# Most of the modulation weights moved from the prologue to beside the first products and the feed-forward, and the norms' roots taken per token and spread through PSUM

## The reference, cut to what matters

```python
def rmsnorm(x, g):
    return x * rsqrt(mean(x * x, axis=-1) + EPS) * g

m = silu(cond) @ ada_w + ada_b                  # ada_w is 1024 x 6144, per layer
sh1, sc1, g1, sh2, sc2, g2 = split(m, 6)
h = rmsnorm(x, norm1) * (1 + sc1) + sh1
x = x + g1 * mixer(h)       # layer 0: gated DeltaNet and pooling, layer 1: Hyena
h = rmsnorm(x, norm2) * (1 + sc2) + sh2
x = x + g2 * conv_glu(h)
...
def conv_glu(h):                                # ffn_up is 1024 x 5632
    a, gte = split(h @ ffn_up, 2)
    a = dwconv_grid(a, ffn_conv_w) + ffn_conv_b
    return (gelu(a) * gte) @ ffn_down
```

## Time and profile before

| | us |
|---|---|
| median of three runs | 4694.48 |
| lowest and highest | 4691.84, 4698.06 |
| the profiled execution | 4689.33 |
| its span, first to last instruction | 4687.5 |

### The profile page before, as it was taken

How to read it: one execution, slowest core, us unless ns; L and a number is a source line. 1 busy time by engine, 2 the same in 40 slices (tenths; PEclk the granted TensorE clock), 3 DMA queues, 4 the chain that set the end, 5 groups by cost and what they waited for, 6 DMA issues and landing times.

```text
span 4687.5 us, 50772 instructions
## 1 busy us (share of the span) xinstructions
PE 4110.0 (88%) x21784; PEld 3429.5 (73%) x21784; DVE 2458.4 (52%) x2646; ACT 1017.6 (22%) x1384; POOL 1178.8 (25%) x586
## 2 busy tenths in 40 slices
PE   6699888778697999999959999996677799999998
PEld 3488777777475888888747777775566588888886
DVE  1466155555416444455447666579992454444453
ACT  1234122211213111111133333311111311111112
POOL 1221133333233222222231000012231422222224
PEclk8799799999798999999979999998888899999999
DMA  9511000000111111111122222232221011111111
GB/s 351 206 52 37 33 1 1 1 1 1 72 37 36 37 41 36 41 36 37 36 78 65 83 80 87 80 144 83 100 111 36 23 37 36 37 37 41 38 39 63
DMA packets 265336, 280.44 MB, mean 60 GB/s; under 512 B 9221, under 2 KB 221142, under 8 KB 261623
## 3 DMA queue, kind: packets, MB, share of 16 engines
q1 hardware_dynamic: 265112, 277.18, 17.5%
HBM read 219.48 MB, written 57.67 MB: 59 GB/s over the span
## 4 chain that ended last, share of the span: by engine, by line
PE 70%; DVE 19%; DMA 4%; issue 3%; ACT 2%; POOL 1%; SPq 1%; POOLq 0%; DVEq 0%; ACTq 0%
PE PS L590 52%; DVE piece L1470 8%; PE PS L1538 5%; DVE piece L1019 3%; DMA piece<-in_l_ada_w 2%; PE PS L990 2%; PE PS L991 2%; PE PS L986 2%; DVE piece L516 2%; PE PS L1711 1%; PE PS L702 1%; DMA piece<-hyena_tokens 1%; DVE piece L1406 1%; DVE piece L509 1%; DVE piece L1879 0%
## 5 line engine op out<-in xcount | busy, mean ns | idle before, releaser
L590 PE MATMUL PS<-piece,piece 128*128 128x512 f32 (+1 forms) x13824 | 2757.3, 361 | 150.7 <-POOL piece L534 94.5
L590 PEld LDWEIGHTS PS<-piece,piece 128*128 128x128 f32 x13824 | 2304.4, 190 | 600.7 <-issue 160.7
L573 POOL TENSOR_TENSOR piece<-piece,piece 128x1024 fp32r<-128x1024 f32 (+1 forms) x204 | 504.7, 2475 | 2417.9 <-ACT piece L567 2417.9
L1538 PE MATMUL PS<-piece,piece 128*128 128x256 f32 x1920 | 441.3, 392 | 126.1 <-DVE piece L2165 110.8
L1406 DVE SCALAR_TENSOR_TENSOR piece<-piece,piece,piece 128x1024 f32<-128x1024 f32 x352 | 534.9, 1520 | 12.6
L1538 PEld LDWEIGHTS PS<-piece,piece 128*128 128x128 f32 x1920 | 376.4, 197 | 186.1 <-DVE piece L2165 113.6
L1426 DVE SCALAR_TENSOR_TENSOR piece<-PS,piece,piece 128x1024 f32<-128x1024 f32 x224 | 187.7, 879 | 415.0 <-PE PS L590 415.0
L567 ACT ACTIVATE piece<-piece 128x1024 fp32r<-128x1024 f32 (+1 forms) x204 | 205.1, 1007 | 671.4 <-PE PS L590 634.5
L1019 DVE TENSOR_TENSOR piece<-piece,PS 128x512 f32<-128x512 f32 x288 | 185.3, 684 | 249.6 <-PE PS L991 192.3
L1403 DVE TENSOR_SCALAR piece<-piece,piece 128x1024 f32<-128x1024 f32 x44 | 35.7, 812 | 482.4 <-ACT piece L1367 482.4
L1125 POOL TENSOR_TENSOR piece<-piece,piece 128x512 f32<-128x512 f32 x120 | 159.8, 1345 | 123.9 <-PE PS L986 123.2
(11 more groups left out here) (206 smaller groups left out, 3719.1 us busy)
## 6 DMA issues: line engine op xcount, KB each, us to landing
piece<-in_l_ada_w SPq DMA_DIRECT2D x24, 2048.0 KB, 18.1
piece<-in_l_ffn_up SPq DMA_DIRECT2D x88, 512.0 KB, 3.7
piece<-in_l_w_in SPq DMA_DIRECT2D x44, 512.0 KB, 3.8
piece<-in_l_ffn_down SPq DMA_DIRECT2D x48, 384.0 KB, 3.0
piece<-filters_s SPq DMA_DIRECT2D x8, 2176.0 KB, 10.5
filters_s<-piece SPq DMA_DIRECT2D x64, 256.0 KB, 2.0
hyena_tokens<-piece SPq DMA_DIRECT2D x24, 640.0 KB, 4.0
piece<-hyena_tokens SPq DMA_DIRECT2D x12, 1280.0 KB, 5.7
```

The lines of the kernel that those rows point to most:

```text
L573: eng.tensor_tensor(LO[i % 2][0][:, 0:n], RAW[i % raws][:, 0:n], HI[i % 2][1][:, 0:n], ALU.subtract)\
L590: m = eng.matmul(PS[:, bank + b, 0:n], w, x[:, a:a + n], start=first and n_ == 0, stop=last and n_ == 2)
L1538: m = eng.matmul(PS[:, bank, o * HC:(o + 1) * HC], M[i][o], rhs[i], start=i == 0, stop=i == 1)
```

## The change

**Modulation.** The prologue handles only the four tiles of 512 columns that the first norm needs (shift and scale of layer 0's first part), each behind a token tile of x (2, 5, 7, 9). The next 18 halves of 256 columns (the rest of layer 0 and the first of layer 1) are handled in the first seven tiles of the first mixer, three to a tile: behind its steps 0, 3 and 5 TensorE multiplies one half and turns the half before. ScalarE copies the rows out, SyncE loads into two buffers. The last 44 quarters of 128 columns (the rest of layer 1) are handled in the feed-forward of layer 0, one in each "a" and "g" tile: the rows behind step 1, the turn behind step 6. ScalarE's copy of a quarter's rows stands at the head of its work for that item. The feed-forward's weight ring goes from two raw buffers to one, in both layers. In the first mixer's queue on SyncE the first two weight loads no longer wait for the prologue.

**Norms.** In `norm`, TensorE sums the squares per token (ten matmuls of one column into bank 6), root and reciprocal run on 128 x 10, VectorE multiplies the identity by them to ten diagonal blocks, and TensorE multiplies ones by these, which leaves the reciprocals of all tokens on all partitions, in PSUM, where the multiplies read them. `first_norm` takes the place of the first call: ScalarE squares each token tile of x as it lands and VectorE reduces it, so that the sums per token need no matmuls; its remaining steps are those of `norm`.

```diff
+            SQX = [r.take(D) for _ in range(2)]
...
+                eng.wait_ge(ac.sem, ac.at("square", t))
+                eng.tensor_reduce(SS[:, t:t + 1], SQX[t % 2], AX.X, ALU.add).then_inc(*ve.did("sum", t))
...
             def high_channels(eng, t):
+                eng.wait_ge(s_x[t % slots], 16 * (t // slots + 1))
+                if t >= 2:
+                    eng.wait_ge(ve.sem, ve.at("sum", t - 2))
+                eng.activation(SQX[t % 2], XR[t % slots], ACT.Square).then_inc(*ac.did("square", t))
...
+        NA, LANES = 4, 4
+        ADA_BEHIND = (2, 5, 7, 9)
...
+                for t in ((0, 1, 2), (3, 4, 5), (6, 7), (8, 9))[n]:
+                    x_fetch(sp, t)
+                src = A["l0_ada_w"].rearrange("(p k) n -> p k n", k=KD)[:, :, n * 512:(n + 1) * 512]
...
+            for t in range(NT):
+                x_turn(pe, t)
+                if t in ADA_BEHIND:
+                    n = ADA_BEHIND.index(t)
+                    rows(n)
+                    if n:
+                        columns(n - 1)
+            columns(NA - 1)
...
+            ve.tensor_tensor(MOD[:, 0, 0:16], PS[:, 4, 0:32].rearrange("p (m j) -> p m j", j=2), bcast(vec("l0_ada_b", 0, 16), 2), ALU.add)\
+                .then_inc(*veM.did("mod"))
+            ve.wait_ge(veM.sem, veM.at("mod"))
+            ve.tensor_scalar(SCALE_A[:, 0], MOD[:, 0, 8:16, :], 1.0, None, ALU.add).then_inc(*veM.did("plus"))
+            ve.wait_ge(veM.sem, veM.at("plus"))
+            ve.tensor_tensor(SCALE_A[:, 0], SCALE_A[:, 0], bcast(vec("l0_norm1", 0, 8), 2), ALU.mult).then_inc(*veM.did("scale"))
+            ve.tensor_copy(SCALE_A[:, 4], bcast(vec("final_norm", 0, 8), 2)).then_inc(*veM.did("last"))
...
-            RS = r.take(N)
+            DIAG, SS, RS = r.take(NT, P), SQ[1][:, 0:NT], psum(3, N)
...
+                for t in range(NT):
+                    m = eng.matmul(PS[:, 6, t:t + 1], SQ[0][:, t * P:(t + 1) * P], ones[:, 0:1], start=True, stop=True)
+                m.then_inc(*pe.did("sum"))
+                eng.wait_ge(ve.sem, ve.at("diag"))
                 for b, (a, n) in enumerate(CHUNKS):
-                    m = eng.matmul(PS[:, b, 0:n], ones, SQ[0][:, a:a + n], start=True, stop=True)
-                m.then_inc(*pe.did("sum"))
+                    m = eng.matmul(PS[:, 3 + b, 0:n], ones, DIAG[:, a // P:(a + n) // P, :].rearrange("p t c -> p (t c)"), start=True, stop=True)
+                m.then_inc(*pe.did("spread"))
...
-                eng.wait_ge(pe.sem, pe.end())
-                eng.activation(RS, psum(0, N), ACT.Sqrt, scale=1.0 / D, bias=eps).then_inc(*ac2.did("root"))
+                eng.wait_ge(pe.sem, pe.at("sum"))
+                eng.activation(SS, PS[:, 6, 0:NT], ACT.Sqrt, scale=1.0 / D, bias=eps).then_inc(*ac2.did("root"))
...
-                eng.reciprocal(RS, RS).then_inc(*ve.did("inv"))
+                eng.reciprocal(SS, SS).then_inc(*ve.did("inv"))
                 eng.wait_ge(ve.sem, ve.at("inv"))
+                eng.tensor_tensor(DIAG, over(ident, NT), bcast(SS, P), ALU.mult).then_inc(*ve.did("diag"))
+                eng.wait_ge(pe.sem, pe.at("spread"))
...
+        def first_norm(prev, shift, early):
+
+            T = [Region(W_AT + i * N, W_AT + (i + 1) * N).take(N) for i in range(4)]
+            DIAG = Region(FIX_AT - N, FIX_AT).take(NT, P)
+            RS = psum(3, N)
...
+            NB, PER, ADA_TILES = 2 * (13 - NA), 3, 7
+            BW = [Region(W_AT + 5248 + 2048 * i, W_AT + 5248 + 2048 * (i + 1)).take(KD, 256) for i in range(2)]
+            BR = [Region(W_AT + 9344 + 256 * i, W_AT + 9344 + 256 * (i + 1)).take(256) for i in range(2)]
...
+            def fetch_half(eng, h):
+                if h >= 2:
+                    eng.wait_ge(peB.sem, peB.at("rows", h - 2))
+                layer, m = divmod(NA + h // 2, 12)
+                at = m * 512 + h % 2 * 256
+                eng.dma_start(BW[h % 2], A[f"l{layer}_ada_w"].rearrange("(p k) n -> p k n", k=KD)[:, :, at:at + 256]).then_inc(s_aw[h % 2], 16)
+
+            def half_rows(eng, h):
+                eng.wait_ge(s_aw[h % 2], 16 * (h // 2 + 2))
+                if h >= 2:
+                    eng.wait_ge(acBr.sem, acBr.at("rows", h - 2))
+                for k in range(KD):
+                    lane = k % LANES
+                    m = eng.matmul(PS[32 * lane:32 * lane + 32, 6 + h % 2, 0:256], CW[:, k, :], BW[h % 2][:, k, :], start=k < LANES, stop=k >= KD - LANES)
+                m.then_inc(*peB.did("rows", h))
+
+            def half_columns(eng, h):
+                eng.wait_ge(acBr.sem, acBr.at("rows", h))
+                for j in range(2):
+                    c = 256 + 4 * (h // 2) + 2 * j
+                    m = eng.matmul(PS[:, 6 + h % 2, c:c + 2], BR[h % 2][:, j * P:(j + 1) * P], SEL, start=True, stop=True)
+                m.then_inc(*peBt.did("turn", h))
+
+            def half_leaves(eng, h):
+                eng.wait_ge(peB.sem, peB.at("rows", h))
+                if h >= 2:
+                    eng.wait_ge(peBt.sem, peBt.at("turn", h - 2))
+                eng.activation(BR[h % 2], PS[:, 6 + h % 2, 0:256], ACT.Copy).then_inc(*acBr.did("rows", h))
...
-                ended(eng, *before_norm)
                 for i, (kind, g, at) in enumerate(tiles):
                     ring.load(eng, i, w_in[:, :, at:at + P], (KD, P))
+                    if i >= 2:
+                        for h in halves(i - 2):
+                            if h + 2 < NB:
+                                fetch_half(eng, h + 2)
                     if i == 1:
+                        ended(eng, *before_norm)
+                        fetch_half(eng, 0)
+                        fetch_half(eng, 1)
...
-                    m.then_inc(*pe.did("used", i))
+                        if k == KD - 1:
+                            m.then_inc(*pe.did("used", i))
+                        h = {0: 0, 3: 1, 5: 2}.get(k)
+                        if h is not None and PER * i + h <= NB:
+                            h += PER * i
+                            if h < NB:
+                                half_rows(eng, h)
+                            if h:
+                                half_columns(eng, h - 1)
...
+                    for h in halves(i):
+                        half_leaves(eng, h)
+                    if i == ADA_TILES - 1:
+                        ended(eng, peB, peBt)
...
+                    if 4 + i == ADA_TILES - 1:
+                        modulation(eng)
...
-            ring = weight_ring(r, len(items))
+            ring = weight_ring(r, len(items), 1)
...
+            NQ, Q_CHUNK = (2 * KH, 4) if layer == 0 else (0, 0)
+            if NQ:
+                QW, QR = r.take(KD, P), [r.take(P) for _ in range(2)]
...
+            def quarter(kind, j):
+                return 2 * j + (kind == "g")
...
+                    if i and items[i - 1][0] in "ag" and NQ:
+                        q = quarter(*items[i - 1][:2])
+                        if q:
+                            eng.wait_ge(peQ.sem, peQ.at("rows", q - 1))
+                        at = (Q_CHUNK + q) * P
+                        eng.dma_start(QW, A["l1_ada_w"].rearrange("(p k) n -> p k n", k=KD)[:, :, at:at + P]).then_inc(s_aw[2], 16)
...
+                            if k == KD - 1:
+                                m.then_inc(*pe.did("used", i))
+                            q = quarter(kind, j)
+                            if k == 1 and NQ:
+                                eng.wait_ge(s_aw[2], 16 * (q + 2))
+                                for kk in range(KD):
+                                    lane = kk % LANES
+                                    m = eng.matmul(PS[32 * lane:32 * lane + 32, 6 + q % 2, 0:P], CW[:, kk, :], QW[:, kk, :], start=kk < LANES, stop=kk >= KD - LANES)
+                                m.then_inc(*peQ.did("rows", q))
+                            if k == KD - 2 and NQ:
+                                eng.wait_ge(acQ.sem, acQ.at("rows", q))
+                                at_ = P + 2 * (q // 2)
+                                eng.matmul(PS[:, 6 + q % 2, at_:at_ + 2], QR[q % 2], SEL, start=True, stop=True).then_inc(*peQt.did("turn", q))
...
+                    if kind in "ag" and NQ:
+                        q = quarter(kind, j)
+                        eng.wait_ge(peQ.sem, peQ.at("rows", q))
+                        if q >= 2:
+                            eng.wait_ge(peQt.sem, peQt.at("turn", q - 2))
+                        eng.activation(QR[q % 2], PS[:, 6 + q % 2, 0:P], ACT.Copy).then_inc(*acQ.did("rows", q))
...
+                    if kind == "d" and j == len(GROUPS_OF) - 1 and mp == 0 and NQ:
+                        eng.wait_ge(peQt.sem, peQt.end())
+                        for odd in range(2):
+                            out = MOD[:, 1, Q_CHUNK:48].rearrange("p (a b) j -> p a b j", b=2)[:, :, odd]
+                            bias = vec("l1_ada_b", Q_CHUNK, NQ).rearrange("p (a b) -> p a b", b=2)[:, :, odd]
```

(39 more changed lines are left out.)

149 lines of the change are left out of this document (108 added, 41 removed).

## The result

The changed kernel takes **4801.07 us** (median of four runs, 4798.23 to 4811.16) beside 4696.27 for the kernel before: ratio **1.0227** (95% interval 1.0208 to 1.0245), slower. The forecast was 4781 us. The profiled execution, 4811.16 us, is the longest of the four, 10 us above their median.

The account below looks back on a forecast made before the run. TensorE was taken to bound layer 0's feed-forward, weight loads the prologue. Prologue and mixer -77, other norms -16.4, feed-forward +180 make +87 on 4689.33, 4776; the runs' median lies 5.2 higher, hence 4781 us, range 4735 to 4825.

Parts of the forecast that it names:

- The sign: Whole kernel: slower, chance 0.93; if layer 0's feed-forward pauses are under 2.6 us per "g" tile, faster instead.
- third rival: Layer 0's feed-forward: the "g" copies are in time and TensorE never stands; 4637 us, chance 0.05.
- The clock: Layer 0's feed-forward: TensorE's clock falls after each pause, adding 1.7 us per hidden tile.
- first rival: Layer 0's feed-forward: the clock holds through the pauses, 37 us less, 4744 us; chance 0.22.
- The row of 3.07 us idle: Filter stage before the change: 32 matmuls took 8.86 us after 3.07 idle, 7.17 after 1.75; basis of the 1.7.
- The halves behind the pooling constants: First mixer: SP holds transfers behind its wait for the constants, two halves come 2 to 3 us late; +4 us.
- Prologue: Start of kernel: first multiplication of the first norm at 64.1 in place of 180.17; -116 us.
- first tile: First projection tile: TensorE stands at the third half until some 11.8 us after the norm; +15.5 us.
- norms: Norm bodies and shifts come sooner: -3.3 us in the first norm, -16.4 in the three later ones.
- Layer 1's feed-forward: Layer 1's feed-forward stays as before; 0 us.
- rivals two and four: Two: small matmuls are dear, 4820 us, chance 0.10. Four: one raw buffer delays down items, 4829 us, chance 0.05.

Follow-up runs that it names:

- The early copy: Changed kernel with ScalarE's copy of each "g" quarter moved ahead of the gelu: 4646.46 us, ratio 0.9904 to the kernel before.
- the pause filled: Changed kernel with 36 unused matmuls of 256 columns ahead of the wait in each "g" quarter: 4751.66 us, ratio 1.0127 to the kernel before.
- the constants later: Changed kernel with the loads of the pooling constants one projection tile later on SyncE's queue: 4786.08 us, ratio 1.0203 to the kernel before.
- alone: Kernel before with only the new norm, in all four places: 4656.58 us, ratio 0.9923.
- two more moves: Changed kernel with early "g" and first-quarter copies, later pooling constants, and first tile's copies and fetches ahead of the norm's end: 4615.61 us, ratio 0.9839.
- the second trace of the changed kernel: Changed kernel timed again without edits, beside the repair of its first tile: 4803.94 us, ratio 1.0249 to the kernel before.

## Why the prediction was right, point by point

**The sign** hung on the pause of the "g" tiles, and that was read from the right place: rows that the kernel before left harmless. The turn behind gelu's copy came 17.6 us after the "a" tile's evacuation (forecast 17.8 after the tile's end), the gate was multiplied 21.7 after it (forecast 19.85 and the clock's 1.7). The early copy shows the cause, and the third rival's price with it: forecast 4637, measured 4646.

**The clock.** The first rival's price was 4744; with the pause filled it is 4752. The forecast's choice against it was right, but its term is the one that was mis-sized in the feed-forward. From the first "a" tile's evacuation to the last, 21 hidden tiles later, it was 841.4 us and is 1035.2, so 9.2 more a tile in place of 8.35: 18 of the 20 us missing there. The pauses were 4.6 (101.6 by 22) instead of 5.0, two quarters 1.9 instead of 1.6, and the clock took 2.4 (53.6 by 22; in the tile shown 8.16 - 5.49 = 2.7) instead of the 1.7 of the earlier trace rows; 0.3 is not placed. The row of 3.07 us idle stood at a granted clock of 0.81 for 9 us (trace of the kernel before), the feed-forward's product at 0.63 for 8.1:

```profile
2608.00:2617.00 9.00, 8.69 (x33) 7.37 (x33) 4.22 (x4) 4.67 (x9) 0.00 (x0) 0.81 0.16 61
```

The Trainium skill, page "TensorE: Matmul & The Clock Gate", section "Loop structure matters more than you think", has the array fall to its lower clock when a long wait stands between bursts. The trace agrees, with 0.63 behind the wait (between 0.50, 1.2 GHz, and 1.00, 2.4 GHz) and 1.00 when it was filled.

**The halves behind the pooling constants** are the other mis-sized term, +4 in the sum. The order on SyncE's queue was seen, but three transfers were late and not two, by 2.8 to 6.2 us and not 2 to 3, and the lower clock behind them (8.28 for 5.46) was not in the term. By the two traces of the changed kernel the stage behind its first tile added 50 and 44 us, not 27; with the constants later it added 25, so the term is 19 to 25.

**Prologue, first tile, norms.** -114.4 for -116; +14.3 for +15.5. As forecast, the first tile hung on the third half: it came 12.3 us after the norm's end (103.89; forecast 11.8). The longer stop ahead of it, 9.9 us for ScalarE's copy, was not foreseen; it cost little as long as the half was later still. The three later norms gave 16.6 us (3.4, 5.2 with its mixer, 8.0) where 15.6 stood in the table, alone 24.3; in layer 0's second norm the first quarter's copy, behind the clearing of the pad, took 2.4 us of a wait.

**Layer 1's feed-forward** did not change (865.1 us in both traces, from the first "a" evacuation to the down products of the last group), and a quarter costs 0.94, a half 1.61: rivals two and four fall. What stays open is the delta stage, which the change does not touch: from 866.8 to 878.0 us in the twelve traces. That it was 5.5 us shorter in the trace of the changed kernel is luck, and it hid a part of the two terms that were too small.

## What to carry to other kernels

Small work laid beside a busy engine costs its own time (here 0.94 us a quarter) only if every step of its round trip is ahead of the slow work on the other engines' queues: one copy on the wrong side of a gelu cost 155 us, more than the whole prologue's gain. For each added wait, find where the releasing instruction stands in its own engine's order, and price the clock behind the wait: the nearest row gave 1.7 us here, and it was 2.4. When a change loses, look for the place before dropping it: moving one copy made this one faster than the kernel before, and two more moves brought it to 4616 us.

## What was not expected of the hardware

The loss of clock did not follow the length of the idle time: behind 2.51 us in the first tile 27 matmuls took 5.46 us, behind 2.81 in the next 8.28, behind 4.51 in the feed-forward 8.16, where 5.46 to 5.49 is their time at clock 1.00. In the second trace of the changed kernel 2.28 us were enough:

```profile
123.75 1.07 PE L739 MATMUL PS<-piece,piece 128*32 128x256 f32 x16 [2.28 <-DMA piece<-in_l_ada_w]
...
125.22 7.04 PE L672 MATMUL PS<-piece,piece 128*128 128x512 f32 x27
```

Matmuls whose results nobody reads paid: 36 of them in each pause, and the kernel was 49 us faster. The delta stage, with its short waits, ran at granted clocks between 0.86 and 1.00 (six traces, each cut in six), and moved by 11 us from trace to trace with the same code; a gain of 6 us ahead of it could not be told.
